# Expert weights in a ring of ten 2 MB slots with 16 KB rows, and row tiles for scatter and bias, in an encoder layer with 32 experts

## The reference

```
h = h + W_out( sig(g_a) * P_a(DiffAttn(n)) + sig(g_s) * P_s(BiS5(n)) ),  n = RMSNorm(h)
h = h + CrossAttn(RMSNorm(h), RMSNorm(mem))      # 4 heads, 256 memory tokens
h = h + MoE(RMSNorm(h))                          # top 4 of 32 experts
```

```
hid  = x @ w_e1[e] + b_e1[e]                     # 1024 -> 2048
gate = min(hid[:, :1024], 7);  lin = clip(hid[:, 1024:], -7, 7)
y    = (gate * sigmoid(1.702 * gate) * (lin + 1)) @ w_e2[e] + b_e2[e]   # 1024 -> 1024
out[token] += softmax_weight * y
```

## Time and profile before

| | |
|---|---|
| three timed runs, median | 1381.03 us |
| three timed runs, range | 1378.91 to 1382.51 us |
| span of the profiled execution | 1379.3 us |
| TensorE busy, share of the span | 1325.5 us, 96% |
| VectorE, ScalarE, GpSimd busy | 364.2, 205.7, 111.8 us |
| DMA traffic | 456.70 MB, mean 331 GB/s |
| granted TensorE clock, mean | 0.987 of 2.4 GHz |

### The profile page before, as it was taken

How to read it: one execution, slowest core, us unless ns; L and a number is a source line. 1 busy time by engine, 2 the same in 40 slices (tenths; PEclk the granted TensorE clock), 3 DMA queues, 4 the chain that set the end, 5 groups by cost and what they waited for, 6 DMA issues and landing times.

```text
span 1379.3 us, 16549 instructions
## 1 busy us (share of the span) xinstructions
PE 1325.5 (96%) x6231; PEld 618.8 (45%) x6231; DVE 364.2 (26%) x799; ACT 205.7 (15%) x311; POOL 111.8 (8%) x107
## 2 busy tenths in 40 slices
PE   7997999999889999999999999999999999999997
PEld 3476886868643333333333333333333333333332
DVE  6389683021142111211111211111211111121112
ACT  2021332100310111111111111111111111111111
POOL 3599100000110000000000000000000000000000
PEclk9998999999989999999999999999999999999999
DMA  8533373449826999999999999999999999999993
GB/s 233 165 122 122 112 120 123 153 138 375 304 84 264 411 416 414 414 417 414 418 412 417 414 415 417 414 418 412 416 413 416 417 414 414 416 416 413 418 413 143
DMA packets 110577, 456.70 MB, mean 331 GB/s; under 512 B 9041, under 2 KB 11169, under 8 KB 87985
## 3 DMA queue, kind: packets, MB, share of 16 engines
q1 hardware_dynamic: 107312, 449.75, 82.4%
q0 software_dynamic: 2080, 5.99, 2.7%
q10 hardware_dynamic: 1152, 0.52, 0.2%
HBM read 454.09 MB, written 1.61 MB: 330 GB/s over the span
## 4 chain that ended last, share of the span: by engine, by line
PE 80%; SPq 5%; DMA 5%; DVE 4%; ACT 3%; issue 1%; ACTq 0%; DVEq 0%
PE pt L899 26%; PE pt L939 15%; PE pt L868 7%; PE pt L517 7%; PE pt L504 6%; DMA ring<-in_w_e 4%; PE pt L552 4%; PE pt L856 4%; SPq L258 4%; PE pt L905 3%; PE pt L484 2%; PE pt L565 2%; ACT wi_ L975 1%; DMA stage<-in_w_in 1%; SPq L267 1%
## 5 line engine op out<-in xcount | busy, mean ns | idle before, releaser
L899 PE MATMUL pt<-ring,stage 128*64 128x512 f32 x1408 | 312.1, 593 | 2.8 <-DMA ring<-in_w_e 2.4
L939 PE MATMUL pt<-ring,wi_ 128*64 128x512 f32 x1024 | 226.8, 595 | 11.6 <-ACT wi_ L975 11.6
L899 PEld LDWEIGHTS pt<-ring,stage 128*64 128x64 f32 x1408 | 101.1, 137 | 205.0 <-issue 192.5
L939 PEld LDWEIGHTS pt<-ring,wi_ 128*64 128x64 f32 x1024 | 70.7, 137 | 147.1 <-issue 127.9
L868 PE MATMUL pt<-stage,uT_ 128*128 128x512 f32 x256 | 115.3, 593 | 0.7 <-ACT stage L975 0.7
L1518 DVE COPY stage<-stage 128x2 f32 (+1 forms) x33 | 5.6, 169 | 386.3 <-PE pt L899 381.2
L1572 DVE TENSOR_SCALAR hnt<-pt 128x512 f32<-128x512 f32 x32 | 22.1, 692 | 278.8 <-PE pt L899 278.8
L1135 ACT ACTIVATE hnt<-hnt 128x512 f32<-128x512 f32 x32 | 20.2, 630 | 466.2 <-DVE hnt L1572 466.2
L868 PEld LDWEIGHTS pt<-stage,uT_ 128*128 128x128 f32 x256 | 46.1, 190 | 47.5 <-issue 45.9
L504 PE MATMUL pt<-stage,hnt 128*128 128x512 f32 x128 | 57.1, 607 | 6.4 <-DMA stage<-in_w_in 4.7
L856 PE MATMUL pt<-a,stage 128*64 128x512 f32 x264 | 62.8, 596 | 0.0
(11 more groups left out here) (317 smaller groups left out, 1257.2 us busy)
## 6 DMA issues: line engine op xcount, KB each, us to landing
ring<-in_w_e SPq DMA_DIRECT2D x304, 1024.0 KB, 17.2
stage<-in_w_e SPq DMA_DIRECT2D x64, 512.0 KB, 14.9
stage<-in_w_in SPq DMA_DIRECT2D x16, 1024.0 KB, 5.6
a<-in_w_e SPq DMA_DIRECT2D x32, 512.0 KB, 15.5
t<-in_w_e SPq DMA_DIRECT2D x32, 512.0 KB, 15.2
stage<-in_w_xkv SPq DMA_DIRECT2D x8, 1024.0 KB, 5.6
ct_<-in_w_e SPq DMA_DIRECT2D x16, 512.0 KB, 15.3
big<-in_w_e SPq DMA_DIRECT2D x16, 512.0 KB, 14.7
```

What stands on the lines that cost most here:

```text
L899: last = pe.matmul(pt[PC][SLOTS * g:SLOTS * (g + 1), 512 * b:512 * (b + 1)], xT[:, k % 4, k // 4], w1_cols(par, k, D * b + 512 * g), start ...
L939: last = pe.matmul(pt[PD][SLOTS * n:SLOTS * (n + 1), 512:1024], hT[:, k % 4, k // 4], w2[:, k, 512 * n:512 * (n + 1)], start=(k == 0), sto ...
```

## The change

- The expert weights go through one ring of ten slots of 2 MB (`ring_slot`): six in `ring`, two in `low` (a1, t1, t2 and t3 put together), two in `stage`. One expert is four chunks of w_e1 and two of w_e2, so the pattern repeats every five experts (`ROUND`), and the loops on SyncE and TensorE are written out for five blocks.
- A partition now receives 16 KB that lie together in HBM: two neighbouring rows of w_e1 (2p and 2p+1 of a group of 256) or four of w_e2. The order in which the products are summed changes with it. So xn (and the router's weights and gains) and hact are written in a permuted order, by strided views in instructions that were there already.
- The loads go strictly in the order of use. Expert 0 is loaded where it was; of expert 1 four chunks (8 MB) are loaded before the loop, not five of 1 MB; the third and the fourth wait for the last slabs of `stage` to be used.
- The scatter uses 64-row tiles: half n of the results on rows 64n to 64n+63, with a selection of these rows only. The zero bands go, and `selw` needs two transposes, not four. The ScalarE copy of `gsc` is 256 columns, not 512.
- The expert bias uses 32-row tiles: the four pieces of 512 columns of the bias table lie on four groups of 32 partitions, with a one-hot `ecol` on each.
- Also moved: the routing tables to ct_, `ysb` and `be2` to big, `xgn` and `xT` to hres, the final result to hnt; some zeroing falls away, and the final gain is loaded at the loop's start.

```diff
-        def load_w1(eng, e, k, par=0):
-            src = w1_dram[0, k] if e is None else w1_dram[bass.ds(e, 1), k].rearrange("a p n -> p (a n)")
-            if par and k < AHEAD:
-                for c in range(2):
-                    eng.dma_start(odd[k][c], src[:, D * c:D * (c + 1)]).then_inc(s_w1[1][k], 16)
-            else:
-                eng.dma_start(w1[:, k, :], src).then_inc(s_w1[0][k], 16)
+        w1_dram = T["w_e1"].rearrange("a e (j p r) n -> (a e) j p (r n)", p=P, j=W1_CHUNKS)
+        w2_dram = T["w_e2"].rearrange("a e (g p c) n -> (a e) g p (c n)", p=P, g=W2_CHUNKS)
+
+        ring_slot = [ring[:, CHUNK * i:CHUNK * (i + 1)] for i in range(6)]
+        ring_slot += [low[:, 0:CHUNK], low[:, CHUNK:2 * CHUNK], stage[:, CHUNK:2 * CHUNK], stage[:, 0:CHUNK]]
+
+        def chunk_at(q, r, j):
+
+            n = CHUNKS * r + j
+            return n % RING, (q * (CHUNKS * ROUND // RING) + n // RING + 1) * 16
+
+        def load_chunk(eng, e, r, j):
+
+            n = (CHUNKS * r + j) % RING
+            dram, c = (w1_dram, j) if j < W1_CHUNKS else (w2_dram, j - W1_CHUNKS)
+            src = dram[e, c] if isinstance(e, int) else dram[bass.ds(e, 1), c].rearrange("a p n -> p (a n)")
+            eng.dma_start(ring_slot[n], src).then_inc(s_chunk[n], 16)
...
+            def load_block(e, q, r, first=0):
+
+                for j in range(first, CHUNKS):
+                    back, was = divmod(CHUNKS * r + j - RING, CHUNKS)
+                    if was < W1_CHUNKS:
+                        sp.wait_ge(m_w1u, W1_CHUNKS * (q * ROUND + back) + was + 1)
+                    else:
+                        sp.wait_ge(m_w2u, W2_CHUNKS * (q * ROUND + back) + was - W1_CHUNKS + 1)
+                    load_chunk(sp, e, r, j)
...
             sp.wait_ge(S["xtp"], 2)
             sp.wait_ge(S["xop"], 2)
-            load_ahead(1, 1, 1, used=False)
+            load_chunk(sp, 1, 1, 0)
+            load_chunk(sp, 1, 1, 1)
+            sp.wait_ge(s_used, len(SLOT_USES) - 2)
+            load_chunk(sp, 1, 1, 2)
+            sp.wait_ge(s_used, len(SLOT_USES))
+            load_chunk(sp, 1, 1, 3)
+            load_block(1, 0, 1, first=RING - CHUNKS)
...
             def scatter(stop, tiles=range(NT)):
+
                 for t in tiles:
                     for n in range(2):
-                        last = pe.matmul(pt[(PA, PB)[t]][:, 512 * n:512 * (n + 1)], gsc[:, n, t], ysb, start=False, stop=stop)
+                        last = pe.matmul(pt[(PA, PB)[t]][:, 512 * n:512 * (n + 1)], gsc[SLOTS * n:SLOTS * (n + 1), t],
+                                         ysb[SLOTS * n:SLOTS * (n + 1), :], start=False, stop=stop)
...
+                for j in range(W1_CHUNKS):
+                    n, loaded = chunk_at(q, r, j)
+                    pe.wait_ge(s_chunk[n], loaded)
+                    for k in (2 * j, 2 * j + 1):
                         for b in range(2):
                             for g in range(2):
-                                pe.matmul(pt[PC][SLOTS * g:SLOTS * (g + 1), 512 * b:512 * (b + 1)], ecol,
-                                          be1[:, D * b + 512 * g:D * b + 512 * (g + 1)], start=False, stop=False)
+                                c = 2048 * (k % 2) + D * b + 512 * g
+                                last = pe.matmul(pt[PC][SLOTS * g:SLOTS * (g + 1), 512 * b:512 * (b + 1)], xT[:, k % 4, k // 4],
+                                                 ring_slot[n][:, c:c + 512], start=(k == 0), stop=(k == KD - 1))
+                        if k == 0:
+                            for b in range(2):
+                                for g in range(2):
+                                    i = NE * (2 * b + g)
+                                    pe.matmul(pt[PC][SLOTS * g:SLOTS * (g + 1), 512 * b:512 * (b + 1)], ecol[i:i + NE, :],
+                                              be1[i:i + NE, :], start=False, stop=False)
+                    last.then_inc(m_w1u, 1)
...
-                for n in range(2):
-                    for t in range(NT):
-                        last = turn(pt[PD][:, 512 + P * (NT * n + t):512 + P * (NT * n + t + 1)],
-                                    selw[:, t, SLOTS * (1 - n):SLOTS * (3 - n)])
+                for t in range(NT):
+                    last = turn(pt[PD][:, 512 + P * t:512 + P * (t + 1)], selw[:, t].rearrange("p n s -> p (n s)"))
...
-                copy(gsc_flat, pt[PD][:, 512:1024]).then_inc(m_gs, 1)
+                copy(gsc_flat, pt[PD][:, 512:512 + NT * P]).then_inc(m_gs, 1)
...
-                dve.tensor_tensor(hact, hgl, hsg, ALU.mult).then_inc(m_act, 1)
+                by_row = (x.rearrange("p (q c) -> p q c", c=4) for x in (hgl, hsg))
+                dve.tensor_tensor(hact.rearrange("p (c q) -> p q c", c=4), *by_row, ALU.mult).then_inc(m_act, 1)
...
-            dve.memset(part(1104, NT * 3 * SLOTS), 0.0)
-            dve.memset(gT, 0.0)
...
+            pool.wait_ge(m_x, 1)
+            pool.dma_start(gfin, T["norm_final_g"].rearrange("(a n) -> a n", a=1).broadcast_to([P, D])).then_inc(s_gf, 16)
```

More of the change, by code:

```diff
@@ L298, in build, with part @@
-        nbx = part(3072, 2)[0:NE]
-        blk = part(3080, 2 * EXTRA + 1)[0:NE]
+        ysb = big[:, 0:512]
+        gsc_flat = lamb[:, 0:NT * P]
+        gsc = gsc_flat.rearrange("p (t l) -> p t l", t=NT)
+        def part(a, n):
+            return ct_[:, a:a + n]
+        ecol = part(0, SLOTS)
+        selw = part(64, NT * 2 * SLOTS).rearrange("p (t n s) -> p t n s", t=NT, n=2)
+        sel = part(320, NT * SLOTS).rearrange("p (t s) -> p t s", t=NT)
+        posn = part(448, NT * NE).rearrange("p (t e) -> p t e", t=NT)
@@ L300, in build @@
+        nbx = part(868, 2)[0:NE]
+        blk = part(870, 2 * EXTRA + 1)[0:NE]
+        gT = lam8[0:NE, 0:L]
+        wr = uT_[:, 0:KD * NE].rearrange("p (k e) -> p k e", k=KD)
+        brt = uT_[:, KD * NE:(KD + 1) * NE]
+        be1 = uT_[:, (KD + 1) * NE:(KD + 1) * NE + 512]
+        be2 = big[0:NE, 0:D]
+        gffn = wi_[:, :]
+        gfin = hres[:, D:2 * D]
+        final = hnt[:, :].rearrange("p (t n) -> p t n", t=NT)
         p2 = a1[:, :].rearrange("p (h t l) -> p h t l", h=HEADS, t=NT)
@@ L330, in _ @@
                     sp.wait_ge(S["ytp"], 1)
-                    for k in range(KD):
-                        load_w1(sp, None, k)
-                    for k in range(KD // 2):
-                        load_w2(sp, None, k)
-            def load_ahead(it, e, par, used=True):
-                for k in range(AHEAD):
-                    if used:
-                        sp.wait_ge(m_w1u, KD * (it - 2) + k + 1)
-                    load_w1(sp, e, k, par)
-                    if not used and k == 2:
-                        sp.wait_ge(s_used, len(SLOT_USES) - 2)
@@ new lines, in _ @@
+            load_chunk(sp, 1, 1, 1)
[4 more added lines that the diff above has]
+            load_block(1, 0, 1, first=RING - CHUNKS)
+            for r in range(2, ROUND):
+                load_block(r, 0, r)
+            with sp.Fori(1, ROUNDS) as q:
+                for r in range(ROUND):
+                    load_block(q * ROUND + r, q, r)
+            for r in range(NE % ROUND):
+                load_block(ROUNDS * ROUND + r, ROUNDS, r)
@@ L934, in block_of @@
                 pe.wait_ge(m_gs, it + 1)
-                for k in range(KD):
-                    if k % 2 == 0:
-                        pe.wait_ge(s_w2[k // 2], 16 * (it + 1))
-                    for n in range(2):
-                        last = pe.matmul(pt[PD][SLOTS * n:SLOTS * (n + 1), 512:1024], hT[:, k % 4, k // 4],
-                                         w2[:, k, 512 * n:512 * (n + 1)], start=(k == 0), stop=(k == KD - 1))
-                    if k % 2:
-                        last.then_inc(m_w2u, 1)
-            block_of(0, 0, first=True)
-            block_of(1, 1)
-            with pe.Fori(1, NE // 2) as pair:
-                block_of(pair * 2, 0)
-                block_of(pair * 2 + 1, 1)
+                for g in range(W2_CHUNKS):
+                    n, loaded = chunk_at(q, r, W1_CHUNKS + g)
+                    pe.wait_ge(s_chunk[n], loaded)
+                    for c in range(4):
+                        for h in range(2):
+                            last = pe.matmul(pt[PD][SLOTS * h:SLOTS * (h + 1), 512:1024], hT[:, c, g],
+                                             ring_slot[n][:, D * c + 512 * h:D * c + 512 * (h + 1)],
+                                             start=(g == 0 and c == 0), stop=(g == 1 and c == 3))
+                    last.then_inc(m_w2u, 1)
+            for r in range(ROUND):
+                block_of(r, 0, r, first=(r == 0))
+            with pe.Fori(1, ROUNDS) as q:
+                for r in range(ROUND):
+                    block_of(q * ROUND + r, q, r)
+            for r in range(NE % ROUND):
+                block_of(ROUNDS * ROUND + r, ROUNDS, r)
             pe.wait_ge(S["ovi"], 1)
@@ L951, in _ @@
             with pe.If(n_extra > 0):
-                with pe.Fori(0, (EXTRA + 1) // 2) as pair:
```

(7 more changed lines are left out.)

184 lines of the change are left out of this document (68 added, 116 removed).

## The result

The changed kernel takes 1338.18 us (median of four runs, 1336.52 to 1338.43) against 1380.88 before: ratio 0.9688 [0.9674, 0.9701], 42.7 us less. Two later series of five runs gave 1337.98 and 1335.45 (0.9706 [0.9684, 0.9727] and 0.968 [0.9656, 0.9705]). The forecast was 1337, with a range of 1322 to 1366. The profiled span is 1336.3 us; 1335.9 was worked out.

A forecast was written before the change was run, and what follows sets the result against it. TensorE bound the kernel, DMA 2 to 3% behind; with the change DMA sets the end. 426.4 + 1.4 + 0.6 + 890.3 = 1318.7, then TensorE's tail to a span of 1335.9, timed 1337 us, range 1322 to 1366.

The forecast's parts named there:

- Which resource ends last: Expert loop: TensorE binds before, DMA 2 to 3% behind; after the change DMA sets the end.
- Part 1: TensorE's expert block: row tiles for scatter and bias and two fewer transposes cut the period from 29.51 to 27.19 us.
- Rival C: Scatter and bias on TensorE: row tiles don't overlap, TensorE binds again, 1370 to 1383 us; chance 0.06.
- without part 1: Expert loop without TensorE's savings: at 29.3 us a block TensorE would still end at about 1368.
- Part 2: Expert-weight queue: a fixed cost per row sets the rate; 16 KB rows give 428.7 GB/s, up from 415.
- Part 3: Expert loads around loop start: 20.97 MB ready instead of 17.8, 381.68 MB left, traffic restarting at 426.4.
- The gap at the fifth slot: Early loop loads: the fifth slot is free only at about 445, a gap of 1.4 us, once.
- The restart: Queue at loop start: first slot free after 4.4 us of block 0, at 424.4, so traffic starts at 426.4.
- the final gain: Its 0.5 MB load on the GpSimd queue moves into the restart of expert loads, costing an estimated 0.6 us.
- The end: After the loop's loads: last chunk landed at 1318.7, last w1 9.8 earlier, w2 done 1324.7, 10.7 behind it, 0.5 for a signal.
- D: TensorE's clock in the loop halves during waits for DMA, some 54 us a block; three blocks give 1412; chance 0.05.
- E: Expert loads: long contiguous rows are slower; below 409 GB/s nothing is gained, at 395 the time is 1413; chance 0.03.

The follow-up runs named there:

- tiles alone: The kernel before, with row tiles for scatter and bias only, old loads and four transposes of selw: 1373.94 us, ratio 0.9952.
- the ring alone: The changed kernel with scatter and bias over the full array again and four transposes of selw: 1380.56 us, ratio 1.0002 to the kernel before.
- the unpermuted rows: The changed kernel with each slot loaded in natural row order, w_e1 in 8 KB and w_e2 in 4 KB rows, one DMA per slot: 1363.3 us.
- 8 KB rows: The changed kernel with each slot's DMA cut by columns into two of 8 KB rows: 1355.13 us, ratio 0.9818 to the kernel before.
- the 4 KB kernel: The changed kernel with each slot's DMA cut by columns into four of 4 KB rows: 1395.28 us, ratio 1.009 to the kernel before.
- less preload: The changed kernel with expert 1's third and fourth chunks waiting until block 0's first chunk is used: 1347.29 us, ratio 0.9752 to the kernel before.

## Why the prediction was right

**Which resource ends last.** Right, and the two single-part runs show it: the queue does. Before, both resources were within 3% of each other, so that tiles alone met the queue (415 GB/s, 45 us of waits), and the ring alone met TensorE (29.51 us a block).

**Part 1.** The period was 27.27 for a forecast of 27.19. The terms: scatter 1.92 for 1.72, bias 1.01 for 0.93, and 0.40 had been set aside for changes of tile shape, of which 0.28 shows inside these two and 0.20 in small amounts elsewhere (the transposes of `selw` 0.37 for 0.27, for one). Row tiles overlap as column tiles do. Rival C is out. The side remark that the kernel "without part 1" would end at 1368 was wrong by 9.6 us, as the span of that kernel is 1377.6. It took 29.3 us a block, but two of the transposes belong to part 1; the period stays 29.51, which is 6.7 us of the 9.6. Another 1.8 is block 0, which starts at 421.86 there and not at 420.03.

**Part 2.** The fit through three row lengths, 2.295 + 0.6 / KB, gave 428.7 GB/s for the fourth; 428 came. It also gave the rates of the unpermuted rows and of 8 KB rows within 1 GB/s. It holds for 4 KB only in the first half of the loop (409), and then misses by 6 GB/s. The prediction's share of about 30 us for the row length comes out as 28 (919.7 us for 381.68 MB at 415 GB/s, 891.8 at 428).

**Part 3.** The gap at the fifth slot is 4 x (428 - 397 + 428 - 303) / 428 = 1.46 us in 440 to 448, for 1.4. The restart is 2.2 us earlier than the 426.4 forecast: by 428, 0.784 + 0.524 + 0.820 = 2.13 MB are in, less 0.52 for the final gain, 3.75 us at full rate, so from 424.2. That is the early block 0, a term that I hadn't seen, and the final gain lies before the restart and costs nothing there (0.6 saved). The 3.14 MB more that lie ready are worth about 7 us, as forecast: less preload shows 8.7 to 9.3 us for 4.19 MB.

**The end, where a size was off.** With an earlier start and the final gain out of the way the loads should have ended 2.8 us sooner than forecast. The rate, 428 for 428.7, takes back 1.5, so by the mean rate they end at 1317.4 and not at 1318.7. The time is the same because another term was mis-sized. I counted a chunk as landed when the mean rate had carried its bytes. The bytes left at 1316 (0.59 MB) give these 1317.4, so the last w1 chunk, 9.8 us ahead, would be in at 1307.6. The chain of the changed kernel says otherwise:

```profile
1267.59 42.62 DMA stage<-in_w_e
1310.21 0.04 issue
1310.25 3.65 PE pt L872 x16
```

It lands at 1310.21, 2.6 us behind the mean. The spread behind that stands in the trace: a chunk counts as loaded when its semaphore has got all of its sixteen increments, and the trace keeps the time of each. For this chunk the first comes at 1306.96, the fourteenth at 1309.02, the last two at 1310.01 and 1310.21. Over the chunks of the loop the last comes 3.24 us after the first (median; 3.4 and 3.5 in the other two profiles of this kernel). So the sixteen shares of a chunk are not carried in step, and the taper at the end of the loads (279, 197, 98 GB/s) is the same spread. The signal itself costs 0.04 us, not 0.5. So the terms of the tail are: landing 1310.21 for 1308.9 (+1.3), signal -0.46, w1 with mid part and w2 15.85 for 15.75 (+0.1), and the part behind the last w2 10.2 for 10.7 (-0.5): together +0.4, which is 1336.3 for 1335.9. From the span to the time it is 1.9 us (1338.22 for 1336.3), where 1.7 less 0.65 had been reckoned. Two errors of some 2.6 to 2.8 us with opposite signs, the early start of the queue and the late landing, stand behind an agreement of 1 us. The size of the effect was understood; that closeness was luck.

**Rivals D and E.** E is out: longer contiguous rows paid at each doubling. The clock (D) did not fall behind a wait in any of the three profiles of the changed kernel. Its waits came to 2.07 us a block by the starts, for a forecast of 2.15, but split in two, and none is longer than 1.44 by the starts (1.3 by the idle times). It did fall inside the loop in one of the three, in block 0 and in dense work. The prediction had named a drop inside the loop as a sign of being wrong. This one costs 3.2 us and isn't what the rival described, a drop behind the waits. I had argued from one wait of 2.53 us that left the clock at 1.00, and the 4 KB kernel shows drops behind each of its five waits of 2.16 to 2.19 us in the loop, with none behind its waits of 1.47. The margin was thinner than a chance of 0.05 says, but the price was lower: a drop there costs 1.7 us and not the 25 us of a whole block that the rival reckoned with.

## What to carry to other kernels

When two resources are within a few per cent of each other, a change to one of them measures little, and neither single part of a combined change tells what the pair is worth: 0.5% and 0.0% alone, 3.1% together. Rates of windows in which one row length is in flight, taken from the profile before, gave a line here that could be extended to the next row length. Where a queue sets the end, count what is loaded before it is needed, and count a chunk as landed when the last of its sixteen increments is there, here 2.6 us behind the mean rate. Compare profiles from the point where the stage in question starts: ahead of it these differed by up to 5.9 us.
